# Moving the activation buffers from 192 to 256 bytes past the weights' 512-byte grid

## The reference

```python
for l in range(DEPTH_2):
    h = _rmsnorm(x, attn_norm_g[l])
    proj = h @ w_in[l]                       # 2048 -> 6144
    ...
    x = x + jnp.concatenate([attn, conv], axis=-1) @ w_out[l]
    hm = _rmsnorm(x, mlp_norm_g[l]) @ w_up[l]          # 2048 -> 8192
    x = x + jnp.square(jax.nn.relu(hm)) @ w_down[l]    # 8192 -> 2048
```

## Time and profile before

| | us |
|---|---|
| median of 3 runs | 3527.8 |
| the three runs | 3525.92, 3527.8, 3557.52 |
| profiled execution, its own time | 3554.12 |
| its span in the trace | 3552.4 |
| PE busy in it | 3354.6 (94%) |
| PEld, DVE, ACT, POOL busy | 3159.5, 1895.6, 1432.0, 403.4 |
| mean granted TensorE clock | 0.974 |

### The profile page before, as it was taken

The page is one execution under the profiler, slowest core; times in us unless marked ns, Lnnn a source line. Parts: engine busy times, 40 slices in busy tenths (PEclk is TensorE's granted clock), DMA queues, the critical chain, the costliest instruction groups (busy, mean ns, idle before and its releaser), DMA issues.

```text
span 3552.4 us, 64645 instructions
## 1 busy us (share of the span) xinstructions
PE 3354.6 (94%) x26228; PEld 3159.5 (89%) x26228; DVE 1895.6 (53%) x2298; ACT 1432.0 (40%) x1868; POOL 403.4 (11%) x425
## 2 busy tenths in 40 slices
PE   7899999998998989989899999998999899999999
PEld 2588888887887979989899999998998899999999
DVE  4755555553566875554544454555555544444444
ACT  5433333332333345543443434334554344343433
POOL 0022222222000410002110001020000210010100
PEclk9999999998999989999999999999999999999999
DMA  8611111110222944444455555554444455555544
GB/s 316 240 48 47 47 47 47 47 47 25 84 83 73 354 154 172 171 167 167 164 189 195 195 189 193 198 189 166 166 174 150 160 189 187 182 187 189 182 184 154
DMA packets 79875, 543.62 MB, mean 153 GB/s; under 512 B 8325, under 2 KB 12437, under 8 KB 15264
## 3 DMA queue, kind: packets, MB, share of 16 engines
q1 hardware_dynamic: 74064, 514.88, 39.6%
q0 software_dynamic: 3040, 20.24, 1.5%
q10 hardware_dynamic: 2672, 7.07, 0.5%
HBM read 537.94 MB, written 4.22 MB: 153 GB/s over the span
## 4 chain that ended last, share of the span: by engine, by line
PE 79%; DVE 9%; issue 6%; ACT 3%; POOL 1%; DMA 1%; DVEq 0%; ACTq 0%; POOLq 0%
PE bank L387 22%; PE bank L388 22%; PE bank L389 22%; PE bank L600 8%; DVE w_lo L371 2%; ACT w_hi L366 2%; DVE gate_acc L1604 1%; PE bank L643 1%; DVE hbuf L1644 1%; PE bank L652 1%; POOL g_M L522 1%; DVE g_acc L1303 1%; PE bank L606 1%; DVE s_acc L1303 1%; PE bank L750 0%
## 5 line engine op out<-in xcount | busy, mean ns | idle before, releaser
L371 DVE TENSOR_TENSOR w_lo<-raw,w_hi 128x2048 fp32r<-128x2048 f32 x477 | 1096.1, 2298 | 933.1 <-ACT w_hi L366 923.3
L366 ACT CAST w_hi<-raw 128x2048 fp32r<-128x2048 f32 x477 | 910.1, 1908 | 608.4 <-PE bank L389 568.6
L387 PE MATMUL bank<-a_lo,w_hi 128*128 128x256 f32 (+1 forms) x3664 | 1089.2, 297 | 12.8 <-DVE a_lo L1584 5.3
L388 PE MATMUL bank<-a_hi,w_lo 128*128 128x256 f32 (+1 forms) x3664 | 1074.6, 293 | 0.0
L389 PE MATMUL bank<-a_hi,w_hi 128*128 128x256 f32 (+1 forms) x3664 | 1073.8, 293 | 0.0
L387 PE MATMUL bank<-h_lo,w_hi 128*128 128x256 f32 x3584 | 1011.5, 282 | 29.6 <-DVE h_lo L1638 20.6
L388 PE MATMUL bank<-h_hi,w_lo 128*128 128x256 f32 x3584 | 999.6, 279 | 0.0
L389 PE MATMUL bank<-h_hi,w_hi 128*128 128x256 f32 x3584 | 999.5, 279 | 0.0
L387 PEld LDWEIGHTS bank<-a_lo,w_hi 128*128 128x128 f32 x3664 | 693.8, 189 | 33.9 <-issue 6.0
L389 PEld LDWEIGHTS bank<-a_hi,w_hi 128*128 128x128 f32 x3664 | 697.2, 190 | 20.3
L387 PEld LDWEIGHTS bank<-h_lo,w_hi 128*128 128x128 f32 x3584 | 677.2, 189 | 39.4 <-issue 16.7
(11 more groups left out here) (308 smaller groups left out, 2639.8 us busy)
## 6 DMA issues: line engine op xcount, KB each, us to landing
raw<-stream SPq DMA_DIRECT2D x485, 1024.0 KB, 4.8
gate_raw<-stream POOLq DMA_DIRECT2D x16, 1024.0 KB, 7.6
xr<-x_t SPq DMA_DIRECT2D x4, 1024.0 KB, 16.4
turned<-by_distance POOLq DMA_DIRECT2D x1, 2048.0 KB, 13.9
x_res<-x_t ACTq DMA_DIRECT2D x1, 2048.0 KB, 22.0
bias_table<-bias ACTq DMA_DIRECT2D x1, 2048.0 KB, 14.4
bias<-bias_table ACTq DMA_DIRECT2D x1, 2048.0 KB, 8.8
out_t<-x_res SPq DMA_DIRECT2D x4, 512.0 KB, 5.1
```

Of the source, the lines that this page charges most:

```text
L366: act.copy(w_hi[u.slot][:], raw[u.raw][:]).then_inc(hi_ready, 1)
L371: dve.tensor_tensor(w_lo[u.slot][:], raw[u.raw][:], w_hi[u.slot][:], ALU.subtract).then_inc(lo_ready, 1)
L387: pe.matmul(acc, wh, lo[:, k, 0:n], start=(k == first), stop=False)
L388: pe.matmul(acc, wl, hi[:, k, 0:n], start=False, stop=False)
```

## The change

`SKEW` becomes 64, and 64 bytes are left free ahead of `shared`.

```diff
-SKEW = 48
+SKEW = 64
...
         pars = put("pars", (N_PAR + 7) // 8 * 8)
         mods = put("mods", 96)
         cols = put("cols", 8)
+        top["at"] += 4 * 16
         shared = top["at"]
```

## The result

The change makes the kernel slower: 3636.7 us in the middle of four runs (3636.1 to 3638.6), against 3542.7 for the kernel before in the middle of its four (3525.9 to 3557.9). The ratio is 1.0268, with a 95% interval from 1.0204 to 1.0331. I had forecast 3527 us and no change, with a range up to 3618. The measured time lies above that range. The 3542.7 is no time of any run: two of the four runs of the kernel before took 3526 and 3528 us and two took 3558, and its middle falls between the pairs.

A forecast was written before the change was run, and what follows sets the result against it. TensorE's start-to-start matmul pace was taken to bound the kernel. From 3554.1 us profiled, zeros for other engines, fp32 and unit matmuls, less 27.6 for one slow MLP, gave 3526.5, said as 3527; range 3440 to 3618.

The forecast's parts named there:

- the 0.84 us to spare: In one unit of layer 1's MLP, `w_lo` is done at 3004.77 and the unit using it begins to load at 3005.61.
- Zero for VectorE and GpSimd: Engines other than TensorE: their buffers move by 64 bytes too, bounded at 1 or 2 ns in 420 to 614; taken as 0.
- zero for the fp32 matmuls: TensorE's fp32 matmuls: scan operands move together and the rows show no dear pair; taken as 0.
- The two rhythms: TensorE's 256-column matmuls in the MLPs: quick at 113.2 ns between starts, slow at 117.6; a slow MLP costs 27.6 us.
- The free pace of 107 ns: TensorE's 256-column matmul at 2.4 GHz without loss, half of 0.215 us at half clock; 6 or 11 ns are lost.
- I take 0 as the change of pace within a rhythm, by the first stage's rows.: The 21744 unit matmuls: distance 192 to 256 bytes costs 0, since the first stage kept 0.230 to 0.235 us through many distances.
- Rival A: Unit matmuls: the repeat divides 256, so 256 is as bad as 0 and all run slow; 3618 us, chance 0.22.
- a further step, at 3710: Unit matmuls of 256 columns: another 4.5 ns on top of the slow rhythm, 92 us more; some 0.08 for beyond 3618.
- The fp32 pairs at 111 ns: Eight fp32 matmuls, both operands at the same offset modulo 512, take 111 to 112 ns each; cited against the slower rival.
- Rival B: Unit matmuls: with a 512-byte repeat, 256 is the greatest distance and streams no longer meet; 3486 us, chance 0.21.
- Rival C: MLPs: the distance chooses quick or slow rhythm, pace within each stays; both slow 3582 us (+1.5%), chance 0.07 in slow form.
- The Trainium skill's rule: TensorE's two SBUF read ports, moving operand and weight load, are independent, so the offset is indifferent; some 3527 us.

The follow-up runs named there:

- the first experiment: Against the kernel before, the whole arena stands 64 bytes higher, so `a` and `h` are at 256 by address but still 192 from the weight halves; 3583.4 us.

## Why the prediction was wrong

**What held.** In the MLPs only the distance between the starts of TensorE's matmuls set the end: the units' other chain stayed hidden. The prediction gave every unit the 0.84 us to spare that it had read in one unit of an MLP, and in the attention that was not so: TensorE had waited for `w_lo` there, and its slower pace took up 7 us of such waits. Zero for VectorE and GpSimd held, by the groups shown above, and zero for the fp32 matmuls by the products of the earlier trace rows, where eight still take 0.90 and 0.89 us. The two rhythms and their price of 27.6 us per MLP held; the kernel of the first experiment, with two slow MLPs, came out at 3583.4, where 3582 was said. The free pace of 107 ns was reached by no kernel.

**The step that failed** is this one: "I take 0 as the change of pace within a rhythm, by the first stage's rows." Those rows have the same 20 ns of loss with 4 columns of weights as the unit matmuls have with 128, and I read that as a loss of the moving stream in which the distance has no part. The result shows why it was no evidence: the first stage kept its pace when its own distances changed by 64 bytes, and the unit matmuls of 512 columns did not (0.233 to 0.227 us). In place of the zero stand 6.7 ns for each matmul of 256 columns over the quick rhythm and 2.2 over the slow one, and 6 ns less for each of 512. The first stage's loads of 4 columns are listed at 90 ns each, the others at 190, so the same 20 ns may well have come about in two ways; what makes them in the first stage was not tested. That the weights have a part in the pace at 256 bytes is shown by the run that moves only `w_lo`, and the runs with shorter loads agree with it.

**The evidence that I had and set aside** were the two rhythms at equal addresses. I wrote that "some give and take between the streams remains" and still took zero. A give and take that is worth 4.5 ns when only the start differs should have made a shift of one stream against the other a real cost.

**Rival A had the mechanism** ("the repeat divides 256"), at a chance of 0.22, and missed in size: it took the slow rhythm, 117.8 ns and 3618 us, as its price, but 256 has a pace of its own, 120.0 ns. It had named a further step, at 3710, and that was too dear, since the true one over the slow rhythm is 2.2 ns and not 4.5. By the pace it should have been 20448 x 6.7 = 137 us over an all-quick run less 8 for 512 columns; the measured 3636.7 is 110 over 3527, since the short stretches of before had been slow in part already (some 11 us of it) and the waits for `w_lo` took up 7. The range ended at A's price, and so 19 us under the result. The fp32 pairs at 111 ns, which spoke against A, speak only for fp32 operands.

**Rival B** (half a period apart) named the period wrongly, and even 128, half of the true period, is bad: 118.6 and 120.0 ns. **Rival C** fails at 256, where the pace is another one and the same in both MLPs: no choice of rhythm was seen there. At 64 and 320 something like it showed, all four MLPs at 117.8 ns with short stretches at 113.3 before them, but two executions can't tell that from luck.

**The Trainium skill's rule** (page "SBUF — State Buffer", section "Who interferes with whom") of two independent read ports gave, as I read it, an indifferent offset. That reading does not hold for these `fp32r` streams at full clock: nine distances gave paces from 113.3 to 120.0 ns with a granted clock of 1.00.

## What to carry to other kernels

When TensorE's start-to-start distance is longer than its free pace and the same instructions show two paces, treat the byte distance between the weights and the moving operand as a setting, and run through a whole period of it (here 256 bytes) in steps of 32; the best place may have bad ones on both sides. A stage with short weight loads was no evidence for one with full loads here. Where a stream can lock into a slow rhythm, look at the spread of the runs as well as at the median, and try whether a few matmuls at another distance bring it out.

## What the runs showed of the hardware

- The pace of `fp32r` matmuls of 256 columns with 128 x 128 weight loads beside them depends on the distance between the two operands modulo 256 bytes: 120.0 ns at 0, 96 and 256, 113.3 or 117.8 at 192, others from 117.3 to 120.0. At half clock the kernel before makes 14 steps from 2427.50 to 2430.49, 213.6 ns each, and half of that is the free pace of some 106.7 ns. The loss over it is 6.7 ns in the quick rhythm and 13.3 at 256, once and twice the same step; the other paces lie between these as if a matmul lost one step in some cases and two in others. That is how the numbers stand to each other, and no run looked into the memory itself.
- What is bad for 256 columns can be good for 512: at 256 bytes these went at 227 ns, at 192 bytes at 233.
- A pace, once taken, holds: in the profiled execution of before, all of layer 1's MLP, some 700 us, ran at 117.8 ns. In one trace two blocks of 16 at another distance ended it, and with one block of 16 no run of 12 had it.
- The fp32 products of the scans kept their pace, and so did the first stage: with `fp32r` weights as the moving operand and 4 columns loaded, 0.230 to 0.235 us, though the distance changed by 64 bytes.
